# A two-layer block with two chunked recurrences: one chunk of 128 tokens per tile in place of two of 64

## The reference

```
# gated delta rule, per chunk; L unit lower triangular, decay from G = cumsum(g)
sol = triangular_solve(I + tril(kb kT * decay, -1), [v*beta, kb*exp(G)]);  u, w = sol
v_new = u - w S
o = (q*exp(G)) S + (q kT * decay) v_new
S = S*exp(G_last) + (k*exp(G_last - G))T v_new          # S = 0 at the start

# hgrn2, per chunk; b = cumsum(log f), k = 1 - f
a[i,j] = sum_d q[i,d] k[j,d] exp(b[i,d] - b[j,d])  for j <= i
o = (q*exp(b)) S + a v
S = S*exp(b_last) + (k*exp(b_last - b))T v              # S = 0 at the start
```

## Time and profile before

| | us |
|---|---|
| median of 3 runs | 1995.29 (1987.48 to 2000.37) |
| profiled execution, its own time | 1986.43 |
| its span | 1984.6 |
| PE busy | 1696.4 (85%) |
| DVE busy | 964.8 (49%) |
| ACT busy | 457.2 (23%) |
| mean granted PE clock | 0.928 of 2.4 GHz |

### The profile page before, as it was taken

How to read it: one execution, slowest core, us unless ns; L and a number is a source line. 1 busy time by engine, 2 the same in 40 slices (tenths; PEclk the granted TensorE clock), 3 DMA queues, 4 the chain that set the end, 5 groups by cost and what they waited for, 6 DMA issues and landing times.

```text
span 1984.6 us, 19743 instructions
## 1 busy us (share of the span) xinstructions
PE 1696.4 (85%) x7864; PEld 1137.9 (57%) x7864; DVE 964.8 (49%) x1781; ACT 457.2 (23%) x1009; POOL 312.4 (16%) x260
## 2 busy tenths in 40 slices
PE   7999988997899578878965776677999999899998
PEld 6857656773585345534632322225998477479953
DVE  3433124422266777545899766664563021546611
ACT  1142123221123344212333422221100012310000
POOL 0000000000001354233344554440000000000000
PEclk9999978998879788889987889989999999899999
DMA  6344211125358889799999999996443433254432
GB/s 243 144 170 170 85 43 43 48 80 180 148 212 339 311 366 424 299 424 424 419 421 378 421 422 421 421 422 256 170 170 130 167 149 134 78 189 167 167 136 106
DMA packets 55193, 471.27 MB, mean 237 GB/s; under 512 B 6592, under 2 KB 7744, under 8 KB 10432
## 3 DMA queue, kind: packets, MB, share of 16 engines
q0 software_dynamic: 36864, 268.45, 33.0%
q1 hardware_dynamic: 18240, 201.60, 27.2%
HBM read 468.98 MB, written 1.05 MB: 237 GB/s over the span
## 4 chain that ended last, share of the span: by engine, by line
PE 60%; DMA 16%; DVE 15%; ACT 4%; issue 3%; POOL 1%; POOLq 0%; DVEq 0%; SPq 0%; ACTq 0%
PE ps L2353 12%; DMA main<-in_expert_uv,main 9%; PE ps L2457 7%; PE ps L442 6%; PE ps L486 5%; DMA panels<-in_expert_uv,main 5%; PE ps L412 4%; PE ps L1228 4%; PE ps L989 4%; DVE main L923 4%; PE ps L2276 3%; PE ps L1460 2%; PE ps L2280 2%; PE ps L2299 2%; DMA panels<-in_wall 2%
## 5 line engine op out<-in xcount | busy, mean ns | idle before, releaser
L905 POOL DMA_INDIRECT main<-in_expert_uv,main x200 | 240.8, 1204 | 940.4 <-DVE main L1794 551.9
L989 PE MATMUL ps<-main 128*128 128x512 f32 x596 | 306.2, 664 | 82.4 <-ACT main L970 79.8
L923 DVE SCALAR_TENSOR_TENSOR main<-main 128x1024 f32<-128x1024 f32 x200 | 240.8, 1223 | 104.3 <-DMA main<-in_expert_uv,main 102.7
L989 PEld LDWEIGHTS ps<-main 128*128 128x128 f32 x596 | 121.4, 213 | 249.3 <-issue 134.3
L2457 PE MATMUL ps<-panels,main 128*128 128x512 f32 x352 | 151.9, 593 | 3.3 <-DMA panels<-in_wall 3.3
L989 PE MATMUL ps<-panels,main 128*128 128x512 f32 x172 | 92.0, 679 | 46.8 <-ACT main L970 40.0
L958 ACT ACTIVATE main<-main 128x2 f32<-128x2 f32 x128 | 26.0, 203 | 437.6 <-DVE main L923 331.9
L442 PE MATMUL ps<-panels,xT 128*128 128x512 f32 x256 | 117.0, 612 | 1.4 <-DVE main L1210 1.4
L2457 PEld LDWEIGHTS ps<-panels,main 128*128 128x128 f32 x352 | 66.6, 190 | 87.2 <-issue 82.3
L2353 PE MATMUL ps<-main 128*128 128x128 f32 x912 | 104.9, 275 | 0.0
L2353 PEld LDWEIGHTS ps<-main 128*128 128x128 f32 x912 | 103.4, 192 | 0.0
(11 more groups left out here) (296 smaller groups left out, 2372.4 us busy)
## 6 DMA issues: line engine op xcount, KB each, us to landing
panels<-in_wall SPq DMA_DIRECT2D x88, 2048.0 KB, 8.1
main<-in_rows SPq DMA_DIRECT2D x14, 512.0 KB, 6.5
...
```

The source lines that it names most:

```text
L905: pool.indirect_dma_start(out=self.bufs[self.buf_of[r]], out_offset=None, in_=self.c.dram["expert_uv"], in_offset=bass.IndirectOffsetOnAxi ...
L923: dve.scalar_tensor_tensor(out=u, in0=u, scalar=1.0, in1=self.c.row(m, H2), op0=ALU.mult, op1=ALU.mult, accum_out=self.dots_at[:, m, q:q + ...
L989: mm = pe.matmul(self.c.ps[:, b, :], self.diags[self.of_pe(r) % DIAG_RING], v[:, half * HALF:(half + 1) * HALF], start=(q == 1), stop=(q = ...
```

## The change

A tile is one chunk. Both recurrences take seven levels. For tile 0 the state is zero before and only made: w, ws, g_cols, q_dec, kb, e_b and the reads of them go, u is copied straight to v_new's place, o is one unit without S, and s is copied by ACT to S. For tile 1 the state is only used: ws, v_new and o are done once for 128 rows, and s, k_dec, to_end and every update of S go. ACT copies o whole, once. The matrices `chunk0` and `chunk1` go, a span and a level matrix come in. In the order, one product with a panel moves from the end of delta 0 into the stage after it, another is put between o and the norm of delta 0 with its read behind the norm, and hgrn of tile 1 has four more steps with two rows each and four rows fewer in its end. Row 76 takes the place of 72. The changes in `hgrn_scalar` and `hgrn_vector` are like those of delta and aren't shown.

```diff
-LEVELS = 6
+LEVELS = 7
...
-MATS = (["ident", "upto", "after", "ones", "chunk0", "chunk1"]
+MATS = (["ident", "upto", "after", "ones"]
...
-    same = p // CHUNK == i // CHUNK
-    out = [p == i, same & (p <= i), same & (p > i), np.ones((P, P)), p < CHUNK, p >= CHUNK]
+    out = [p == i, p <= i, p > i, np.ones((P, P))]
...
-PARTS_FROM = 72
+PARTS_FROM = 76
...
+def delta_units(m):
+
+    units = {"norm": ["norm_k", "norm_q"], "turn": ["k_t", "v_t"], "kk": ["kk", "beta", "qk"], "P0": ["P0"],
+             "decay": ["decay", "g_cols", "g_rows"] if m else ["decay", "g_rows"]}
+    for l in range(1, LEVELS):
+        units.update({f"P{l}": [f"P{l}"], f"XY{l}": [f"X{l}", f"Y{l}"] if l < LEVELS - 1 else [f"Y{l}"]})
+    units.update({"uw": ["u", "w"][:m + 1], "ws": ["ws"] if m else [], "o": ["o"] if m else ["o", "s"]})
+    return units
+
+
+def hgrn_units(m):
+
+    units = {"k_t": ["k_t", "same"], "ends": ["e_b"] if m else ["to_end"], "o": ["o"] if m else ["o", "s"]}
+    for l in range(LEVELS):
+        units.update({f"span{l}": [f"span{l}"], f"a{l}": [f"a{l}"]})
+    return units
+
+
...
-        self.b_diag, self.kb, self.wT, self.u, self.o = self.N_l, self.g_run, self.decay, self.X, self.X
+        self.b_diag, self.kb, self.wT, self.o = self.N_l, self.g_run, self.decay, self.X
...
+        self.u = self.X if m else self.v_new
...
-    act.wait_ge(*un.full(name("g_cols")))
-    act.activation(t.e_cols, un.view(name("g_cols")), ACT.Exp).then_inc(un.freed(name("g_cols")), 1)
+    if m:
+        act.wait_ge(*un.full(name("g_cols")))
+        act.activation(t.e_cols, un.view(name("g_cols")), ACT.Exp).then_inc(un.freed(name("g_cols")), 1)
...
-    act.wait_ge(*un.full(name("w")))
-    act.activation(t.wT, un.view(name("w")), ACT.Copy).then_inc(un.freed(name("w")), 1)
+    if m:
+        act.wait_ge(*un.full(name("w")))
+        act.activation(t.wT, un.view(name("w")), ACT.Copy).then_inc(un.freed(name("w")), 1)
     yield "uw"
-    for ch in range(2):
-        r = rows_of_chunk(ch)
-        yield f"ws{ch}"
-        yield f"o{ch}"
-        act.wait_ge(*un.full(name(f"o.{ch}")))
-
-        act.wait_ge(*un.read_out(name(f"ws.{ch}")))
-        act.activation(t.o[r], un.view(name(f"o.{ch}"))[r], ACT.Copy).then_inc(un.freed(name(f"o.{ch}")), 1)
-        yield f"S{ch}"
-    for ch in range(2):
-        act.wait_ge(*un.read_out(name(f"o.{ch}")))
+    yield "ws"
+    yield "o"
+    if m:
+        act.wait_ge(*un.read_out(name("ws")))
+    act.wait_ge(*un.full(name("o")))
+    act.activation(t.o, un.view(name("o")), ACT.Copy).then_inc(un.freed(name("o")), 1)
+    if m == 0:
+        act.wait_ge(*un.full(name("s")))
+        act.activation(t.S, un.view(name("s")), ACT.Copy).then_inc(un.freed(name("s")), 1)
+    yield "S"
+    act.wait_ge(*un.read_out(name("o")))
...
-            step(dve.tensor_tensor(t.bg, t.beta[:, m, :], t.e_g[:, 0:8], ALU.mult))
-            dve.tensor_tensor(t.kb, t.k_t, along(t.bg, DH), ALU.mult).then_inc(c.up("kb"), 1)
-        if l == 3:
-            dve.wait_ge(*c.at("kb", m))
-            dve.tensor_tensor(t.k_dec, t.k_t, along(t.e_g[:, 8:16], DH), ALU.mult).then_inc(c.up("k_dec"), 1)
+            if m:
+                step(dve.tensor_tensor(t.bg, t.beta[:, m, :], t.e_g[:, 0:8], ALU.mult))
+                dve.tensor_tensor(t.kb, t.k_t, along(t.bg, DH), ALU.mult).then_inc(c.up("kb"), 1)
+            else:
+                dve.tensor_tensor(t.k_dec, t.k_t, along(t.e_g[:, 8:16], DH), ALU.mult).then_inc(c.up("k_dec"), 1)
         yield f"XY{l}"
     yield "uw"
-    dve.wait_ge(*un.read_out(name("u")))
-    for ch in range(2):
-        r = rows_of_chunk(ch)
-        dve.wait_ge(*un.full(name(f"ws.{ch}")))
-        dve.tensor_tensor(t.v_new[r], t.u[r], un.view(name(f"ws.{ch}"))[r],
-                          ALU.subtract).then_inc(un.freed(name(f"ws.{ch}")), 1)
-        yield f"ws{ch}"
-        yield f"o{ch}"
-        dve.wait_ge(*un.full(name(f"o.{ch}")))
-        if m == 0 and ch == 0:
-            dve.wait_ge(*c.at("no_state"))
-        step(dve.tensor_tensor(t.S, t.S, along(t.e_g[:, 16 + 8 * ch:24 + 8 * ch], DH), ALU.mult))
-        dve.wait_ge(*un.full(name(f"s.{ch}")))
-        dve.tensor_tensor(t.S, t.S, un.view(name(f"s.{ch}")), ALU.add).then_inc(un.freed(name(f"s.{ch}")), 1)
-        dve.wait_ge(*un.read_out(name(f"s.{ch}")))
-        yield f"S{ch}"
+    if m:
+        dve.wait_ge(*un.read_out(name("u")))
+        dve.wait_ge(*un.full(name("ws")))
+        dve.tensor_tensor(t.v_new, t.u, un.view(name("ws")), ALU.subtract).then_inc(un.freed(name("ws")), 1)
+    yield "ws"
+    yield "o"
+    yield "S"
...
-    wide("g_cols", ones, t.g_run)
+    if m:
+        wide("g_cols", ones, t.g_run)
...
-    pe.wait_ge(*c.at("kb", m))
-    heads("w", lambda h: t.kb[:, h, :], lambda h: t.Y[:, h, :])
+    if m:
+        pe.wait_ge(*c.at("kb"))
+        heads("w", lambda h: t.kb[:, h, :], lambda h: t.Y[:, h, :])
     yield "uw"
-    pe.wait_ge(*un.read_out(name("w")))
-    pe.wait_ge(*c.at("k_dec", m))
+    pe.wait_ge(*un.read_out(name("qk")))
+    if m:
+        pe.wait_ge(*un.read_out(name("w")))
+        pe.wait_ge(*un.read_out("delta0.s"))
+        heads("ws", lambda h: t.wT[:, h, :], lambda h: t.S[:, h, :])
+    yield "ws"
     if m == 0:
-        pe.wait_ge(*c.at("no_state"))
-    pe.wait_ge(*c.at("q_dec", m))
-    pe.wait_ge(*un.read_out(name("qk")))
-    for ch in range(2):
-        r = rows_of_chunk(ch)
-        heads(f"ws.{ch}", lambda h: t.wT[:, h, :], lambda h: t.S[:, h, :])
-        yield f"ws{ch}"
-        pe.wait_ge(*un.read_out(name(f"ws.{ch}")))
-        pe.wait_ge(*un.emptied(name(f"o.{ch}")))
+        pe.wait_ge(*un.read_out(name("u")))
+        heads("o", lambda h: t.a_qk[:, h, :], lambda h: t.v_new[:, h, :])
+        pe.wait_ge(*c.at("k_dec"))
+        heads("s", lambda h: t.k_dec[:, h, :], lambda h: t.v_new[:, h, :])
+    else:
+        pe.wait_ge(*un.read_out(name("ws")))
+        pe.wait_ge(*c.at("q_dec"))
+        pe.wait_ge(*un.emptied(name("o")))
         for h in range(HEADS):
-            out = un.view(name(f"o.{ch}"))[:, h, :]
+            out = un.view(name("o"))[:, h, :]
             pe.matmul(out, t.q_dec[:, h, :], t.S[:, h, :], start=True, stop=False)
-            mm = pe.matmul(out, t.a_qk[r, h, :], t.v_new[r, h, :], start=False, stop=True)
+            mm = pe.matmul(out, t.a_qk[:, h, :], t.v_new[:, h, :], start=False, stop=True)
         mm.then_inc(un.filled(), 1)
-        heads(f"s.{ch}", lambda h: t.k_dec[r, h, :], lambda h: t.v_new[r, h, :])
-        yield f"o{ch}"
-        yield f"S{ch}"
-        pe.wait_ge(*un.read_out(name(f"s.{ch}")))
+    yield "o"
+    yield "S"
...
-    heads("e_b", lambda h: t.log_f[:, h, :], lambda h: c.mat("upto"))
-
-    pe.wait_ge(*un.emptied(name("to_end")))
-    for b in range(2):
-        mm = pe.matmul(un.view(name("to_end"), 2)[:, b, :], c.mat("after"),
-                       flat(t.log_f)[:, b * HALF:(b + 1) * HALF], start=True, stop=True)
-    mm.then_inc(un.filled(), 1)
+    if m:
+        heads("e_b", lambda h: t.log_f[:, h, :], lambda h: c.mat("upto"))
+    else:
+        pe.wait_ge(*un.emptied(name("to_end")))
+        for b in range(2):
+            mm = pe.matmul(un.view(name("to_end"), 2)[:, b, :], c.mat("after"),
+                           flat(t.log_f)[:, b * HALF:(b + 1) * HALF], start=True, stop=True)
+        mm.then_inc(un.filled(), 1)
     yield "ends"
-    pe.wait_ge(*un.read_out(name("a5")))
-    for ch in range(2):
-        r = rows_of_chunk(ch)
-        if ch == 0:
-            pe.wait_ge(*c.at("q_dec_b", m))
-            pe.wait_ge(*c.at("k_dec_b", m))
-        pe.wait_ge(*un.emptied(name(f"o.{ch}")))
+    pe.wait_ge(*un.read_out(name(f"a{LEVELS - 1}")))
+    if m:
+        pe.wait_ge(*c.at("q_dec_b"))
+        pe.wait_ge(*un.read_out("hgrn0.s"))
+        pe.wait_ge(*un.emptied(name("o")))
         for h in range(HEADS):
-            out = un.view(name(f"o.{ch}"))[:, h, :]
+            out = un.view(name("o"))[:, h, :]
             pe.matmul(out, t.q_dec[:, h, :], t.S[:, h, :], start=True, stop=False)
-            mm = pe.matmul(out, t.a_qk[r, h, :], t.v[r, h, :], start=False, stop=True)
+            mm = pe.matmul(out, t.a_qk[:, h, :], t.v[:, h, :], start=False, stop=True)
         mm.then_inc(un.filled(), 1)
-        heads(f"s.{ch}", lambda h: t.k_dec[r, h, :], lambda h: t.v[r, h, :])
-        yield f"o{ch}"
-        yield f"S{ch}"
-        pe.wait_ge(*un.read_out(name(f"s.{ch}")))
+    else:
+        heads("o", lambda h: t.a_qk[:, h, :], lambda h: t.v[:, h, :])
+        pe.wait_ge(*c.at("k_dec_b"))
+        heads("s", lambda h: t.k_dec[:, h, :], lambda h: t.v[:, h, :])
+    yield "o"
+    yield "S"
...
-        if l == 3:
-            panel(0)
...
-    part("delta0", "ws0", "o0")
-    panel(0)
-    part("delta0", "S0", "ws1", "o1", "S1", "gate")
-    panel(0)
+    part("delta0", "ws", "o", "S")
+    at = next(beside[0])
+    part("beside0", at)
+    part("delta0", "gate")
+    part("read0", at)
     part("hgrn0", "k_t")
```

(40 more changed lines are left out.)

73 lines of the change are left out of this document (35 added, 38 removed), and 4 rows, old and new, of the table DELTA_UNITS.

## The result

| us | before | after |
|---|---|---|
| median | 1996.28 (4 runs) | 1922.14 (1920.09 to 1925.88, 4 runs) |
| profiled execution, its own time | 1986.43 | 1920.09 |
| its span | 1984.6 | 1918.2 |

The ratio is 0.9656, with a 95% interval of 0.9628 to 0.9683. The forecast was 1927, and 1920 for the profiled execution. The runs of the kernel before scatter more than those of the changed one: 1975.7 to 2000.4 us in the 31 runs of all comparisons, against 1917.9 to 1925.9 in ten. So the difference of the medians, 74.1 us, is less sure than it looks; with the eleven runs of before that stood beside the second measurement of the changed kernel it is 69.6. To see whether that came about for the reasons given, I cut the span at instructions that both kernels have.

What follows compares the result with a forecast made beforehand. PE and DVE work before the first gather, then DMA's gather from 720 us, set the pace. -37.9 - 3.6 - 11.4 - 11.6 - 6 + 4 = -66.5: 1920 profiled, 1929 from the median; forecast 1927, range 1903 to 1956.

Steps and rivals of the forecast that it cites:

- Step 1: End of tile 0's delta: hgrn's first transposes come at 257.5 in place of 295.39 us, 37.9 us earlier.
- The new o: PE's o unit, all with 128 rows: bounded by 3.6 and 6.6 us, taken as 3.6.
- Step 2: Hgrn of tile 0 beside delta of tile 1: turn_b 41.5 us earlier, 3.6 more than before this stage.
- rival B: No idle at the gate, none added in tile 1's selection, clock 1 beside hgrn of tile 0: 1909 us; chance 0.11.
- Rival C: PE's clock stays at the lower level from 257 to 412 us, costing 128 us: 2057 us; chance 0.03.
- Step 3: Tile 0's selection: first gather 11.4 us earlier, and 11.6 more by delta's norm starting sooner after row 0.
- Rival A: Second 11.6 us lost to loads of panels, gate's idle stays, tile 1's selection costs the full 10: 1952 us; chance 0.18.
- Steps 4 and 5: Gather, tile 1: 6 us less DMA idle at the gate by hgrn's end, 4 us more in the selection.

Runs made afterwards that it cites:

- o_full: Kernel before, with the second matmul of each head in o taking all 128 rows in place of the chunk's 64; 1954.70 us, ratio 0.9832.
- pad_first: Changed kernel with 16 extra DVE operations of 128x1024 between top0 and best0 of tile 0; 1937.64 us, ratio 0.9737 to before.
- gate80: Changed kernel with PARTS_FROM 80 in place of 76; 1910.72 us, ratio 0.9618 to before; measured again, 1915.00 us, ratio 0.9643.
- fast4: Changed kernel with one row in place of two behind the last four steps of hgrn of tile 1; 1912.18 us, ratio 0.9624 to before.

## Why the prediction held, step by step

**Step 1** was worked out to 37.9 and measured 38.4. That the norm is covered by the moved panel, and that the panel between levels 3 and 4 covered nothing, both held. The clock's part was bounded at 10 us and, by `o_full`, is 9.3. I had tied the fall to PE's waits; `o_full` keeps those waits (1.40, 1.68, 1.39, 1.38 and 1.63 us) and its clock is 1.00 over the stretch, so they don't suffice as a reason. The forecast survived since it was made from durations at the full clock.

**The new o** is 3.7 us, against bounds of 3.6 and 6.6. "The 3 us are off the path where they arise" was said of the new units; that the old ones cost 2.8 us each and 9.3 of clock besides was in the sum as a whole, but I hadn't seen how much of the gain this alone would be.

**Step 2** gave 6.0 in place of 3.6. From XY4 to turn_b it is 3.7, to the point. The other 2.3 lie before XY4 (110.3 us against 112.6), where the granted clock was 0.98 and not 0.95; that I left out, and rival B had it as a clock of 1 throughout. This surplus is chance in part: of the ten traces with this code in step 2, seven took 154.3 us at a mean clock of 0.99 and three 156.1 to 157.5 at 0.96 to 0.97, so the gain lay between 2.8 and 6.0. Rival C's slow clock never came.

**Step 3** gave 12.7 and 12.6 for 11.4 and 11.6. The first surplus lies ahead of o: from turn_b to it PE took 74.3 us where it had taken 75.7, and I had said that nothing changes there. In the second, row 0 landed sooner (5.86 for 7.8 us); but its 12.6 was 10.2 in the second trace of the same kernel, so being 1.0 off says little. Rival A's loads of panels held up PE three times up to row 12, for 4.5 us together, and didn't decide; `pad_first` shows that DVE's chain does.

**Steps 4 and 5** gave 0.7 for 2 (1.6 in the second trace). The idle time fell by 6.2 us at the gate, for 6, and rose by 4.5 in the selection, for 4, so both mechanisms held. The two nearly cancel, and `gate80` and `fast4` show that both could be had. From the first gather's issue to the last sum it takes 793.6 us in place of 806.9: 13.3 less, for the 14 forecast.

**The sum** of the terms was 3.9 us short, and the start of the execution 4.2 us long. The profiled execution of before lay 9.9 us under the median of its four runs; part of that is its start, the shortest of all 14 traces.
